# The even mixer of a two-block kernel rebuilt: head pairs, outputs by features, and products woven between projection and output units

## The reference

```python
h = _rmsnorm(x, mix_norm[layer])
proj = h @ even_w_in[i]                      # 512 z | 1024 xBC | 8 dt | 512 u
y_a = _ssd_mixer(zxbcdt, ...)                # 8 heads of 64, 2 groups, state 128
y_b = _s5_mixer(u, ...)                      # 32 groups of 16 channels, 64 states each
mixed = jnp.concatenate([y_a, y_b], -1) @ even_w_out[i]
x = x + mixed
```

## Time and profile before

| | |
|---|---|
| three runs | 1858.25, 1858.3, 1862.09 us, median 1858.3 |
| the profiled execution | 1863.99 us, its span 1862.1 us |
| mean granted clock of TensorE | 0.943 |
| TensorE busy | 1729.8 us, 93% of the span |
| VectorE, ScalarE, GpSimd busy | 1156.0, 794.7, 225.0 us |
| feed-forward end to last output product of the even mixer | 967.7 to 1156.3 us |

### The profile page before, as it was taken

One profiled execution on the slowest core, in us unless ns is written; L12 is line 12 of the kernel. 1 busy time (PEld: TensorE's weight loads), 2 busy tenths in 40 slices (PEclk: granted clock), 3 DMA queues, 4 the chain that ended last, 5 costly groups with the idle time before them and its releaser, 6 DMA issues.

```text
span 1862.1 us, 29011 instructions
## 1 busy us (share of the span) xinstructions
PE 1729.8 (93%) x11696; PEld 1585.4 (85%) x11696; DVE 1156.0 (62%) x1424; ACT 794.7 (43%) x959; POOL 225.0 (12%) x301
## 2 busy tenths in 40 slices
PE   2999899979998999899989688999999999889998
PEld 2897799968977999799989577999989999779998
DVE  7876877877557444756557573555555556545554
ACT  1654343335443433443444534434354435444442
POOL 3001000000000000189516100000000000300000
PEclk8999899989998999899999668999999999789999
DMA  9945688765544555455644202655546555315652
GB/s 314 332 169 179 215 313 279 266 217 190 193 132 152 186 184 182 122 183 182 201 136 141 86 23 74 203 180 180 181 136 202 177 184 161 112 62 187 202 178 94
DMA packets 221412, 330.11 MB, mean 177 GB/s; under 512 B 6327, under 2 KB 183064, under 8 KB 221342
## 3 DMA queue, kind: packets, MB, share of 16 engines
q1 hardware_dynamic: 206112, 276.91, 44.8%
q0 software_dynamic: 14832, 52.12, 8.1%
q10 hardware_dynamic: 398, 0.11, 0.0%
HBM read 328.03 MB, written 1.09 MB: 177 GB/s over the span
## 4 chain that ended last, share of the span: by engine, by line
PE 71%; DVE 15%; DMA 6%; ACT 4%; issue 3%; SPq 0%; POOLq 0%; DVEq 0%; ACTq 0%; POOL 0%
PE bank L1952 33%; PE bank L1996 20%; PE bank L1984 6%; DMA s_late<-in_w_ada 5%; DVE s_late L1430 4%; PE bank L1965 2%; DVE s_wL L1412 2%; ACT s_wH L1014 2%; DMA s_mix<-in_w_ada 1%; PE bank L2109 1%; DVE s_hL L1447 1%; PE bank L2101 1%; PE bank L2100 1%; DVE s_small L1714 1%; DVE s_mix L547 1%
## 5 line engine op out<-in xcount | busy, mean ns | idle before, releaser
L1412 DVE TENSOR_TENSOR s_wL<-s_raw,s_wH 128x2048 fp32r<-128x2048 f32 x254 | 585.9, 2311 | 349.8 <-ACT s_wH L1014 349.5
L1952 PE MATMUL bank<-s_hH,s_wH 128*128 128x256 f32 x2240 | 641.5, 286 | 12.7 <-DVE s_hL L1460 5.5
L1952 PE MATMUL bank<-s_hL,s_wH 128*128 128x256 f32 x2240 | 638.1, 285 | 0.0
L1952 PE MATMUL bank<-s_hH,s_wL 128*128 128x256 f32 x2240 | 637.9, 285 | 0.0
L1014 ACT ACTIVATE s_wH<-s_raw 128x2048 fp32r<-128x2048 f32 x254 | 484.0, 1907 | 186.3 <-PE bank L1996 127.3
L1952 PEld LDWEIGHTS bank<-s_hH,s_wH 128*128 128x128 f32 x2240 | 434.1, 194 | 18.2 <-issue 15.1
L1952 PEld LDWEIGHTS bank<-s_hL,s_wH 128*128 128x128 f32 x2240 | 434.1, 194 | 2.5 <-issue 0.2
L1952 PEld LDWEIGHTS bank<-s_hH,s_wL 128*128 128x128 f32 x2240 | 434.2, 194 | 0.0
L1996 PE MATMUL bank<-s_wH,s_aH 128*128 128x512 f32 x480 | 187.9, 391 | 0.0
L1996 PE MATMUL bank<-s_wL,s_aH 128*128 128x512 f32 x480 | 187.5, 391 | 0.0
L1996 PE MATMUL bank<-s_wH,s_aL 128*128 128x512 f32 x480 | 186.7, 389 | 0.0
(11 more groups left out here) (445 smaller groups left out, 2263.6 us busy)
## 6 DMA issues: line engine op xcount, KB each, us to landing
s_raw<-in_w_ffn_in SPq DMA_DIRECT2D x44, 1024.0 KB, 5.2
s_raw<-in_ffn_w_gate SPq DMA_DIRECT2D x44, 1024.0 KB, 5.1
s_raw<-in_ffn_w_up SPq DMA_DIRECT2D x44, 1024.0 KB, 5.2
s_raw<-in_ffn_w_down SPq DMA_DIRECT2D x44, 1024.0 KB, 5.0
s_late<-in_w_ada POOLq DMA_DIRECT2D x20, 2048.0 KB, 11.0
s_raw<-in_w_ffn_out SPq DMA_DIRECT2D x22, 1024.0 KB, 5.0
s_raw<-in_w_in_ab SPq DMA_DIRECT2D x12, 1024.0 KB, 11.8
s_raw<-in_w_in_cd SPq DMA_DIRECT2D x12, 1024.0 KB, 8.0
```

The lines of the kernel that those rows point to most:

```text
L1412: TTn(wL[:, slot, :], raw[:, slot, :], wH[:, slot, :].bitcast(F32), ALU.subtract).then_inc(lo_ready, 1)
L1952: last = mm(dst[:, ft * T:ft * T + T], w, h[:, k, :], start=(k == 0 and i == 0), stop=(k == KC - 1 and i == 2))
```

## The change

**Feed-forward layer f1a.** The transposes of the output weights stand before the last full round, and the 32 drive-weight transposes stand within it and the tail, eight after each of four units, through banks 6 and 7. ScalarE copies them after its splits. It also copies the last 32 columns of each drive tile to `SD3`.

**Projection.** The units come in the order xBC (4), u (2), z (2), all column units. ScalarE does the first tap. The lag products stand after unit 1. u is brought to its layout by 64 small TensorE products (`turn_u`) with slices of the identity as weights, instead of ScalarE's 16 copies.

**Scan.** Heads go in pairs. ScalarE computes the argument with Relu out of PSUM (four instructions a pair) and one exp of 768 columns, the mask is multiplied into C.B once, and y comes out with features on partitions (weights of 128 x 64, 256 and 128 columns moving). Pieces of the two z units stand between. The norm's sum over features is made by TensorE with a matrix of ones, and the root and reciprocal are of 128 x 256.

**Recurrence and output.** Drives, local and state products are cut into quarters with 32 columns of weights, so that each writes one quadrant of partitions: 128 drives, 64 local and 128 state products. y then stands with features on partitions in banks 2 and 3, and gelu and the last product read it there. Output units 0 and 1, which need only the scan's y, are woven in between; units 2 and 3 come last. Four gate products share two banks, which gives up the waits between them.

The rest of the diff gives `TURN_BANK` and `SUM_BANK` four banks by name instead of a first one (`o_even` sums in banks 0, 1, 4, 5), moves tiles in the scratch regions `mix` and `t32`, and lets GpSimd load the gate weights after the last y pair.

```diff
-        EVEN_COLS = [0, 256] + [512 + 256 * i for i in range(4)] + [1544, 1800]
+        EVEN_COLS = [512 + 256 * i for i in range(4)] + [1544, 1800, 0, 256]
 def even_pe
+            def turn_u(h):
+                for i in range(8):
+                    q = 32 * (i % 4)
+                    for j in range(CHUNK):
+                        src = by_chunk(uT[:, 2 * h + i // 4, :])[:, :, j]
+                        last = mm(bank[7 - h][32 * j:32 * j + 32, CHUNKS * i:CHUNKS * i + CHUNKS], ident[:, q:q + 32], src,
+                                  start=True, stop=True)
...
+            def decays(p):
...
+                for i in range(2):
+                    last = mm(bank[2 + p % 2][:, T * i:T * i + T], head_bcast(2 * p + i), cumT, start=True, stop=True)
...
+            def y_pair(p):
+                pe.wait_ge(ev("w_done"), p + 1)
...
+                for i in range(2):
...
+                    mm(dst, xdt[:, 0, c], w[:, 0:T], start=True, stop=False, skip_group_check=True)
+                    last = mm(dst[:, P:T], xdt[:, 1, c], w[:, T:3 * P], start=False, stop=True, skip_group_check=True)
...
+            def drives(h):
+                for n in range(8):
+                    for ri in range(2):
+                        for q in range(0, P, 32):
+                            last = mm(bank[6 + ri][q:q + 32, CHUNKS * n:CHUNKS * n + CHUNKS], SD[:, ri, 8 * h + n, q:q + 32],
+                                      uR[:, 8 * h + n, :], start=True, stop=True)
...
+            def local(h):
...
+                for j in range(CHUNK):
+                    for i in range(8):
+                        q, at = 32 * (i % 4), (i // 4 * CHUNK + j) * CHUNKS
+                        mm(bank[2 + h][q:q + 32, at:at + CHUNKS], ML[:, 8 * h + i, 32 * j:32 * j + 32], uR[:, 8 * h + i, :],
+                           start=False, stop=False, skip_group_check=True)
...
+            unit(0)
...
+            narrow(1).then_inc(ev("dt_mm"), 1)
+            row_bc("even")
+            unit(1)
...
+            lags()
+            unit(2)
+            unit(3)
+            unit(4)
...
+            unit(5)
...
+            turn_u(0)
...
+            decays(0)
+            gate_units(0, 6)
...
+            turn_u(1)
...
+            decays(1)
+            gate_units(6, 12)
+            pe.wait_ge(ev("u_turned"), 2)
+            drives(0)
+            gate_units(12, 18)
+            pe.wait_ge(ev("g_mid"), 1)
+            y_pair(0)
+            decays(2)
+            gate_units(18, 26)
+            y_pair(1)
+            decays(3)
+            pe.wait_ge(ev("s5_rot"), 1)
+            drives(1)
+            gate_units(26, 32)
+            y_pair(2)
+            y_pair(3)
+            pe.wait_ge(ev("arg_done"), 4)
+            variances(0)
+            variances(1)
...
+            out_half(0, 0)
+            out_half(0, 1)
...
+            local(0)
+            states(0)
+            out_half(1, 0)
...
+            gates(0)
+            gates(1)
+            out_half(1, 1)
+            local(1)
+            states(1)
+            gates(2)
+            gates(3)
+            pe.wait_ge(tl_ready, 4 * TR["o_even"] + 4)
+            rows_last(o0 + 2, (hH, hL, 4), (hH, hL, 6), name="o_even")
 def even_act, the order from unit 6 on
+            used(6)
+            split_py(n0 + 9)
+            decay(2)
+            decay(3)
+            used(7)
+            split_py(n0 + 10)
+            silu_z(0)
+            silu_z(1)
+            square(0)
+            square(1)
+            deviation(0)
+            upper_part("o_even", 0)
+            deviation(1)
+            upper_part("o_even", 1)
+            split_py(o0 + 3)
+            gelu(0)
+            split_py(o0 + 4)
+            gelu(1)
 def even_dve, the order from the first decay product on
+            decay_product(0)
+            rotate(0)
+            decay_product(1)
...
+            scan(0)
+            y_skip(0)
+            evacuate_z(0)
+            split_py(n0 + 9)
+            decay_product(2)
+            y_skip(1)
+            decay_product(3)
+            evacuate_z(1)
+            split_py(n0 + 10)
+            gated(0)
...
+            y_skip(2)
+            y_skip(3)
+            gated(1)
+            normed(0)
+            lower_part(TR["o_even"], 0)
+            normed(1)
+            lower_part(TR["o_even"], 1)
+            rotate_back(0)
+            rotate(1)
+            scan(1)
+            split_py(o0 + 3)
+            rotate_back(1)
 def ffn (TensorE)
+                elif name == "f1a":
+                    with pe.Fori(1, FC - 2) as i:
+                        body(i)
+                    output_weights()
+                    body(FC - 2, drive_weights)
```

More of the change, by code:

```diff
@@ L366, in even_pe @@
             pe.wait_ge(ev("so_ready"), 1)
-            pe.wait_ge(ev("sd_ready"), 1)
+            pe.wait_ge(ev("sd3"), 1)
             pe.wait_ge(ev("dt_abs"), 1)
             pe.wait_ge(row_ready, RMS["even"] + 1)
-            for n in range(16):
-                m, q = n // 4, 32 * (n % 4)
-                for part, (lo, size) in enumerate(((0, 32), (32, 96))):
-                    for ri in range(2):
-                        rhs = CT0[:, ri, n, :] if part == 0 else SO[:, ri, n, 0:96]
-                        last = mm(bank[7][q:q + 32, m * P + lo:m * P + lo + size], SD[:, ri, n, 96:128], rhs,
-                                  start=(ri == 0), stop=(ri == 1))
@@ L461, in even_act @@
-        def even_act(act_e, A, step, transposed, upper_part):
-            for k in range(4):
+                mm(bank[g][:, 0:T], B[:, 0:P], C, start=True, stop=True)
+                mm(bank[g][:, T:T + P], B[:, P:T], C[:, P:T], start=True, stop=True).then_inc(ev("g_mm"), 1)
+            decays(1)
[6 more added lines that the diff above has]
+            decays(2)
@@ new lines, in silu_z, with square, deviation @@
+            def silu_z(g):
+                act_e.wait_ge(ev("z_scaled"), g + 1)
+                z = zT[:, 2 * g:2 * g + 2, :]
+                A(z, z, ACT.Silu).then_inc(ev("z_silu"), 1)
+            def square(g):
+                act_e.wait_ge(ev("gated"), g + 1)
+                A(zT[:, 2 * g:2 * g + 2, :], t32[:, 2 * g:2 * g + 2, :], ACT.Square).then_inc(ev("sq_ready"), 1)
+            def deviation(g):
+                act_e.wait_ge(ev("var_mm"), g + 1)
+                A(zT[:, 2 * g, :], bank[2 + g][:, 0:T], ACT.Sqrt, bias=eps_rms, scale=1.0 / 256).then_inc(ev("std_read"), 1)
@@ new lines, in gelu @@
+            def gelu(h):
+                act_e.wait_ge(ev("s5_out"), h + 1)
+                for m in (2 * h, 2 * h + 1):
+                    A(by_chunk(gl[:, m, :]), y_rows(m), ACT.Gelu_apprx_tanh).then_inc(ev("gelu_done"), 1)
+            used(0)
+            row_copy("even")
+            split_py(n0 + 3)
+            first_tap(0)
+            used(1)
+            split_py(n0 + 4)
+            first_tap(1)
+            act_e.wait_ge(ev("dt_abs"), 1)
+            step(A(sp8[0], sp8[0], ACT.Exp))
@@ L488, in even_act @@
[L488 to L499 removed]
+            used(2)
@@ new lines, in even_act @@
+            split_py(n0 + 5)
+            first_tap(2)
+            silu_x(0)
+            used(3)
+            split_py(n0 + 6)
+            first_tap(3)
+            silu_x(1)
+            used(4)
+            split_py(n0 + 7)
+            silu_x(2)
+            used(5)
+            split_py(n0 + 8)
+            silu_x(3)
+            copy_u(0)
+            decay(0)
+            copy_u(1)
+            act_e.wait_ge(ev("g_mm"), 2)
+            A(G[:, 0, P:T], bank[0][:, P:T], ACT.Copy)
+            A(G[:, 1, P:T], bank[1][:, P:T], ACT.Copy).then_inc(ev("g_mid"), 1)
@@ L548, in conv @@
+            def conv(k):
+                dve.wait_ge(proj_evac, u0 + k + 1 + EVAC0)
+                dve.wait_ge(ev("tap_done"), k + 1)
+                for tap in range(1, 4):
+                    for c in (2 * k, 2 * k + 1):
+                        w = cols[:, C_CONVW + 8 * tap + c:C_CONVW + 8 * tap + c + 1]
+                        last = STT(xbcT[:, c, :], xpad[:, c, tap:tap + T], w, xbcT[:, c, :], ALU.mult, ALU.add)
                     if tap < 3:
@@ new lines, in even_dve @@
+            dve.wait_ge(ev("sd_ready"), 1)
+            step(dve.memset(xpad[:, :, 0:3], 0.0))
+            for i in range(2):
+                r = slice(HD * i, HD * i + HD)
+                step(dve.tensor_copy(dskc[r, :], dsk.rearrange("p (c i) -> p c i", i=2)[r, :, i]))
+            dve.wait_ge(row_ready, RMS["even"] + 1)
+            evacuate_x(0)
+            dve.wait_ge(ev("dt_mm"), 1)
+            step(TTn(sp8[1], bank[7][0:8, 0:T], rowR[0:8, :], ALU.mult))
+            step(TS(sp8[1], sp8[1], a8[:, 1:2], None, ALU.add))
@@ L629, in even_dve @@
-            transposed("o_even", lambda c: cols[:, C_SSDN + c:C_SSDN + c + 1], groups=2, direct=True)
-            for h in range(2):
-                dve.wait_ge(ev("s5_out"), h + 1)
-                y_back(dve.tensor_copy, h, 0, copy=False)
```

(3 more changed lines are left out.)

638 lines of the change are left out of this document (344 added, 294 removed).

## The result

The changed kernel takes 1812.6 us (median of 4 runs, 1811.5 to 1814.4) where the kernel before takes 1858.3 beside it. The ratio is 0.9742, 95% interval 0.9729 to 0.9755, so 2.6% faster. The forecast was 1813.0, range 1801 to 1834.

A forecast was written before the change was run, and what follows sets the result against it. The even mixer was taken as bound by a chain passing between engines: 131.0 us in place of 188.6, 4.45 more before it, 8 given back, net 45.1 saved; profiled 1818.9, median 1813, range 1801 to 1834.

The forecast's parts named there:

- A: Mixer start, 0 to 14.2 us (before 20.0): x transposed, copied and split, then first unit work, narrow product and row broadcast.
- B: Mixer to 47.4 us, set by TensorE: units 1 to 5, lags and transposes, 33.1 us; VectorE has 28.8.
- C: Mixer to 78.1 us, set by TensorE: gate units, turns, decay broadcasts, G product, drives and y pairs, 30.7 us.
- chain D: Mixer to 88.1 us: serial chain from the z unit's end through splits, silu, gating, norm root and reciprocal, 12.6 us.
- E: Mixer to 116.9 us, set by TensorE: four output halves, local parts, states, gate products, zeros and waits, 28.8 us.
- F: Mixer to 120.1 us: sigmoids, products, upper and lower parts, 3.2 us.
- G: Mixer end, to 131.0 us: the last four output halves, 11.0 us.
- The open price: Small TensorE product, 32 weight columns and 64 moving; the change brings 384, taken at 0.047 us each from the lag products.
- Serial: Rival: small products run one after the other at 0.215 us, 64.5 us more, 1878 us; chance 0.05.
- The doubled price: Rival: small products cost twice the price, 0.1 us, 20.4 us more, 1834 us; chance 0.16.
- Clock lost from D on: Rival: TensorE's later mixer work runs at half clock, 34.7 us more, 1848 us; chance 0.07.
- Weaving not got: Rival: VectorE sets B and C; ten us lost gives 1823, inside the range, counted within the forecast's 0.69.

The follow-up runs named there:

- the repetition: The changed kernel measured once more with no edit: 1811.6 us, ratio 0.9737 to the kernel before.
- quarter by quarter: Changed kernel with the 64 drive products of a half reordered, all 16 of one column quarter before the next: 1822.2 us.
- the filling: Changed kernel plus products of zeros at the norm, 18 ahead of the variances and 20 behind them: 1812.6 us.
- the last order: Changed kernel with ScalarE computing silu of z ahead of the third output unit's weight split, VectorE's half of that split behind the gating: 1808.0 us.
- Outputs last: Changed kernel with the 48 output products of the first two units moved behind all steps of the last gates: 1819.5 us.
- the gate first and all fillings: Changed kernel with silu of z ahead of the split, plus zero products behind the x transposes, around the variances and before the last output: 1806.2 us.
- weights after the layer: Changed kernel with the 8 output-weight and 32 drive-weight transposes and their copies moved behind the feed-forward layer: 1829.8 us.
- whole drives: Changed kernel with a half's drives as 16 products of 128 weight columns instead of 64 of 32: 1814.3 us.

## Why the prediction was right

The code's effect was forecast as 45.1 us with the profiled execution at 1818.9; the medians differ by 45.6. That the two agree to half a microsecond is luck, in two ways. The profiles differ by 49.6, 4.5 more than forecast, and by stages it is 48.0 (49.6 with the repetition). The profile of the kernel before lay 5.7 above its median, which I carried over, and that of the changed kernel only 1.7; the medians of the repetition, measured beside the kernel before, differ by 48.2. And inside the mixer two errors cancel. Small products and y pairs were 6.6 us cheaper than in the sum, and what I gave back as 8 was 11.9: 136.3 measured against 131.0 less 6.6. The mechanism is borne out all the same, as the stages fall where the forecast put them. Step by step, in the forecast's own terms:

| step | forecast | measured |
|---|---|---|
| feed-forward layer | +4.45 | +4.25 |
| A | 14.2 | 15.9; 7.66 and 6.65 for the first unit in other profiles where it took 8.07 here |
| B | 33.1 | 33.2 |
| C, to the last y pair | 30.7 | 29.1 (1018.2 to 1047.3) |
| chain D from the z unit's end | 12.6 | 13.3 (1045.8 to 1059.2) |
| first output half, from the layer's end | 88.1 | 90.1 |
| E | 28.8 | 28.9 |
| F | 3.2 | 3.4 |
| G | 11.0 | 14.0, then 12.8 |
| mixer, 8 given back | 139 | 136.3, then 134.8 |

**The open price.** I took 0.047 and it is 0.030 for 320 of the 384, 0.062 for the other 64: 0.015x64 - 0.017x320 = 4.5 us less than forecast. The y pairs were 0.8 in place of 1.33, 2.1 us less in all; that the two heads' halves of the columns overlap would fit this, and no run isolates it. The rule of the Trainium skill that I set against the row ("TensorE: Matmul & The Clock Gate", section on packing small matmuls) is not borne out as I used it: all products use all 128 rows, and at 0.030 each in four quarters against 0.105 in one they do overlap, by their columns. I had taken one sentence on weight loads for the price of a whole product; the same section of the Trainium skill also lists products in separate column strips as running together, and there the trace agrees with it. The row that argued "the lag products also write quadrants" was right in kind, and the lags' four in a row in one quarter, of which I had made an argument for the new ones, point to what the run quarter by quarter priced with 16 in a row. Serial at 0.215 that run is not either: 0.105.

**The clock.** I gave back 1.6 for each of three starts. By single profiles the costs are 0 to 1.4 at A, 2.2 at the first output unit, 0 to 2.8 at G. The middle one is mostly hidden (the filling there gave 0.5). What reached the end is then some 1.4 + 0.5 + 2.8 = 4.7 in the changed profile and 1.0 + 0.5 + 1.6 = 3.1 in its repetition, an estimate, so my 4.8 was right as a sum for one of the two and wrong in its parts. I had not seen that the same wait can cost anything from nothing up.

**Chain D.** The reciprocal of 128x256 was forecast at 1.7 from columns of 1 and 16, and took 1.75. The order of the chain was right: it had silu, squares, table, root and no variances. I doubted that when I expected a gain from the filling, and the filling confirmed it. What the forecast took as given is that the split stands ahead of the gate; that this is worth 3 us only the last order showed.

**E** came out right for a partly wrong reason. I had it as TensorE's own work, 28.8. Local and state products cost about 3.5 less, the first output unit 2.2 and the other two halves 0.6 more, and there is 1.0 us of a stop. Outputs last shows VectorE close behind: without the 48 products the stretch is still 27.4 us, in 6.8 of which TensorE waits for VectorE.

**The rivals.** The doubled price is what a bad order costs, and this order does not have it. Clock lost from D on: 0.93 in E, so no. Serial: no. Weaving not got: it was got in C, all of whose stretch stood at 1.00, and is worth 5.5 to 7 us there and 4.9 to 6.4 in E. What the change gained beyond that lies in the shorter work itself (heads in pairs, features on partitions) and in the early turning of the weights. The 15 to 18 us of that run are against turning all of them behind the layer, which the kernel before did not do either: it turned the 32 drive tiles between its heads. So how much of the gain over the kernel before each of these three brings was not tried.

## What to carry to other kernels

Price small TensorE products by their neighbours: in this kernel four with 32 columns of weights each, in four quarters in turn, cost 0.12 us together, and 0.42 when they follow each other in one quarter. When a chain crosses engines, look in the waiting engine's own queue for a weight split or a table load that can be passed by work whose data is long ready; here two swapped steps gave 3 us. An idle TensorE has a second price in its clock that one profile shows too high or too low, so take it as a range, and before filling a wait with products of zeros ask whether the work behind it has slack.

## What the runs showed of the hardware that was not expected

A stop of TensorE inside the state products, 1.0 us in the changed profile with nothing that the profile shows as its cause:

```profile
1067.03 1.10 PE L452 MATMUL bank<-s_t,s_gate 128*32 128x64 f32 x64 [0.16 <-issue]
1067.95 1.81 PE L463 MATMUL bank<-s_mix,s_late 128*32 128x63 f32 x114
1070.74 0.42 PE L463 MATMUL bank<-s_mix,s_late 128*32 128x63 f32 x14 [0.98 <-issue]
```

The DMA queues between 1068 and 1069 us:

```profile
q8 instruction: 1, 0.02, 5.7%
```

One packet of 0.02 MB on the instruction queue, and no other traffic. In four profiles such a packet moved in the two microseconds up to the stop (1.0, 1.7, 1.4 and, with the gate first and all fillings, 2.1 us). In seven of the profiles without a filling at the norm the stop, of 1.0 to 1.7 us, stands at the same place of the program, behind 114 of the 128 records of the first half's states. With the weights after the layer it stands there behind 107, and once more in the second half. With the filling at the norm, which adds instructions, it stands in the second half's states alone. So quarter products, with a record every 15 ns, seem to use instructions up faster than they arrive. The Trainium skill, "Runtime: NRT & Kernel Launch", section on instruction fetch mechanics, has fetches hidden because instructions are issued more slowly than they are fetched; if this is the cause, the trace does not agree.

Two runs do not have the stop. The whole drives have 96 products fewer ahead of the states (TensorE, the first half's states):

```profile
1076.01 1.94 PE L462 MATMUL bank<-s_mix,s_late 128*32 128x63 f32 x128
```

With the outputs last TensorE had just waited 5.6 us for VectorE, time in which instructions could arrive. Both fit the reading. But neither run was made for it, and in the whole drives a packet of this kind also moved during the states without a stop. So the cause is argued and not shown.

The second surprise stands above: whole products of 64 float32 columns, back to back with TensorE busy throughout, saw the clock go from 1.00 to 0.50, in one of two halves of one profile.
